# One bank and half the queries for the levels, value products by turns, context tables made earlier

## The chip, the cores and the metric

The kernel runs on one NeuronCore of a Trainium2 chip. The metric is the device time in microseconds, as a median of several executions. The engines named are PE (TensorE, matrix products; PEld is its load of the stationary operand), DVE (VectorE), ACT (ScalarE), POOL (GpSimd) and SP (SyncE, which here only issues transfers). PSUM has eight banks of 128 partitions x 512 fp32 values; the code calls them `ps[:, bank, :]`.

## The reference

What is computed is two blocks on 512 tokens of width 1024. Cut to what matters here:

```python
def first_block(x, c, ctx, ...):
    px = split(modulate(rms_norm(x, norm1), sh1, sc1) @ w_in)       # q, k, v; q, f_fwd, f_bwd, i, g
    pc = split(modulate(rms_norm(ctx, norm1), csh1, csc1) @ w_in)   # the same of 256 context tokens
    na_x = neighbourhood_attention(...)   # 8 heads of 64; window of 8 rows x 16 columns, bias by
                                          # relative offset, one softmax with all context keys
    hg_x = hgrn2_mixer(...)               # 4 heads of 128, forward and backward in time
    x = x + gt1 * (concat(na_x, hg_x) @ w_out)
    return rms_norm(x + gt2 * peer_ffn(modulate(rms_norm(x, norm2), sh2, sc2), ...), norm_f)

def second_block(x, ...):                 # stick-breaking and latent attention, 8 heads each
    proj = (rmsnorm(x, norm_gain) * (1.0 + scale) + shift) @ w_in
    ...

# hgrn2_mixer, per head and direction: decayed linear attention, from a state that the context left
A = einsum('btd,bsd,btsd->bts', q, k, exp(b_t - b_s))   # for s <= t (or >=, backward)
o = A @ v + (q * exp(b)) @ S0                           # S0 = sum over context of k_dec^T v
```

## The kernel before

The program has four functions that run one after the other, each a block of queues for the five engines: `phase_project` (modulation, norm, all projections; 0 to 285 us), `phase_mix` (window attention and the recurrent mixer; 285 to 496), `phase_peer` (output projection, norm, the feed-forward with product keys, the final norm; 496 to 1834), and `second_block` (to the end at 2325). Activations are kept transposed, features on partitions and tokens along the row. Large products are made as three products in fp32r: `split3` (lines 1115 to 1117) multiplies high by high, low by high, high by low part; ScalarE makes the high part, VectorE or POOL the low part. Small ones are plain fp32.

**`phase_project`** streams 32 pieces of the weights; a piece is 8 k-steps of `split3`. The last pieces are those of the gates `g`, whose products ScalarE's sigmoid and VectorE's product (line 413) finish.

**`phase_mix`** has two strands. The attention has 32 items (a head, a block of 16 columns x 8 rows; two heads of a pair follow each other). An item is `scores` (lines 729, 730: 256 window keys, 256 context keys), DVE's bias and maxima (`item`, lines 941, 945), ACT's exponential (894) and scaling (898), `turn` (738: four transposes into bank 2), ACT's copy to `pT` (922), `values` (750: four 64-column products into one half of bank 3). The recurrent strand has four units, `unit` = head pair and direction `d`; a unit has ten levels 0 to 9 and a `read_out`. Level 0 is the diagonal. At level s from 1 to 7 (`LEV`) the tokens of each tile of 128 are cut in runs of 2^(s-1); a query in a later run of a pair meets the keys of the earlier one, through `qd` (made by DVE, line 997), `kd` (POOL, 716) and the running factors `suf` and `fx` (DVE, 1003, 1007). TensorE makes the whole 128x128 matrix for each of 4 tiles and 2 heads (`level`, line 791, one bank a head, 4 and 5), and DVE copies the valid part of it into `A_diag` under a mask (`copied`, 966). Levels 8 and 9 mix whole tiles (808 and below). TensorE's product of level s waits for the copy of level s-1 (`level_cp`), head by head.

Ahead of unit 0 stands, for each direction, `context(d)`: eight transposes of the context's decayed keys `k.fc[d]` (759), ACT's copy to `kcT` (905), eight products with the context's values (765) to the state, ACT's copy of it (908). Three bias tables of 128x2048 (one for the left edge, the inner blocks, the right edge) are made from `k.toep` and `k.mask`: DVE makes the first (1037) and POOL the other two (699).

The order of the mix is set by slots: slot n holds `scores(n)`, then a share of the recurrent steps, spread evenly by `fill` over 36 slots, then `turn(n-2)` and `values(n-3)`. Every engine has the same slots in its queue.

**`phase_peer`** first makes the output projection (`out_part`, banks 0 to 7), adds squares for the norm, and spreads the reciprocal root (`spread_quarters`, line 1131) over the partitions; then groups of two tiles follow, `OUT_G` = 4 the first after the norm. DVE makes h of the norm (1626, 1622) k-step by k-step, which the first tile of group `OUT_G` waits for (`h_split`). After that group TensorE turns h (1412, 1413) and waits for the weights' low part of POOL (1331). At its end DVE adds residuals and squares for the next norm (1800).

**`second_block`** begins with the same kind of norm (`n_inverse`, `n_spread`; h by lines 2416 and 2422), then projects tile by tile from weight pieces (ACT line 2180 high, DVE 2311 low). The rotary angles (`rope_angles`, line 2365) lie in DVE's queue ahead of a low part.

## Time and profile before

| | us |
|---|---|
| median of 3 runs | 2329.17 (2326.9 to 2331.43) |
| the profiled execution | 2327.29 |
| its span on the core | 2325.5, mean clock granted to TensorE 0.977 |
| TensorE busy | 2196.0 (94%) |
| VectorE busy | 1664.4 (72%) |
| ScalarE busy | 908.7 (39%) |
| POOL busy | 624.9 (27%) |

A row of a timeline is: start in us, duration in us, engine, line, operation, out<-in, shapes, xcount (consecutive ones joined), and in brackets the idle time of the engine before it and what ended that. A row by lines is: line, engine, operation, names, shapes, xcount | busy us, mean ns of one | idle us before them and who ended it. A row of a table by stretches is: the stretch in us, its length, busy us of PE, PEld, DVE, ACT and POOL with the number of instructions in brackets, the granted clock of TensorE as a share of full, the share of the DMA engines, GB/s. A product of plain fp32 is two records.

### The profile page before, as it was taken

To read this page: it belongs to the slowest core of one execution; us is meant where nothing else is said; L and a number is where in the kernel's file an instruction comes from. 1 tells how busy PE (TensorE), PEld (TensorE's weight loads), DVE (VectorE), ACT (ScalarE), POOL (GpSimd) and SP (SyncE) were. 2 spreads that over 40 slices of the span, in tenths; PEclk is the share of its full clock that TensorE was granted. 3 is DMA by queue.
4 is the path that set the end of the run, shared out by engine and by line. 5 is a ranking of instruction groups with operands and counts; after the bars stand their busy time and mean duration, and the time that the engine had idled before them with its cause. 6 is when DMAs were issued, how large, how long until landed. Compare 5 with 4: busy or idle time off the path is not lost. (4 is left out here: it accounts for less than half of the span.)

```text
span 2325.5 us, 31686 instructions
## 1 busy us (share of the span) xinstructions
PE 2196.0 (94%) x12605; PEld 1961.9 (84%) x12605; DVE 1664.4 (72%) x2779; ACT 908.7 (39%) x1191; POOL 624.9 (27%) x355
## 2 busy tenths in 40 slices
PE   5999889988999998999999899999999899889997
PEld 3888777866799998999999899999999777667775
DVE  6645677873479999889886788888887645656543
ACT  3322234343233333566663333333333434556432
POOL 0000042322347776333325333333332000000000
PEclk8999999999999999999999999999999999999999
DMA  7677400012237777899999999999998122111222
GB/s 263 216 235 240 163 33 1 1 73 73 91 115 244 248 241 235 314 357 339 353 356 385 356 359 352 358 355 352 359 353 308 68 82 90 55 42 55 78 90 73
DMA packets 177443, 486.13 MB, mean 209 GB/s; under 512 B 13648, under 2 KB 80336, under 8 KB 165776
## 3 DMA queue, kind: packets, MB, share of 16 engines
q1 hardware_dynamic: 140432, 349.87, 43.6%
q0 software_dynamic: 36864, 134.23, 15.5%
q8 instruction: 100, 1.64, 0.3%
q14 instruction: 47, 0.39, 0.0%
HBM read 429.52 MB, written 52.43 MB: 207 GB/s over the span
## 5 line engine op out<-in xcount | busy, mean ns | idle before, releaser
L1115 PE MATMUL ps<-h_high,u_high 128*128 128x384 f32 (+1 forms) x1216 | 427.7, 352 | 19.9 <-POOL u_low L1331 12.4
L1117 PE MATMUL ps<-h_high,u_low 128*128 128x384 f32 (+1 forms) x1216 | 419.7, 345 | 0.0
L1116 PE MATMUL ps<-h_low,u_high 128*128 128x384 f32 (+1 forms) x1216 | 419.6, 345 | 0.0
L1115 PE MATMUL ps<-w_high,v_high 128*128 128x384 f32 x1024 | 344.5, 336 | 7.5 <-DVE w_low L1750 7.5
L1117 PE MATMUL ps<-w_high,v_low 128*128 128x384 f32 x1024 | 343.8, 336 | 0.0
L1116 PE MATMUL ps<-w_low,v_high 128*128 128x384 f32 x1024 | 343.6, 336 | 0.0
L1115 PEld LDWEIGHTS ps<-h_high,u_high 128*128 128x128 f32 x1216 | 230.3, 189 | 33.9 <-POOL u_low L1331 14.6
L1481 ACT ACTIVATE v_high<-v_raw 128x2048 fp32r<-128x2048 f32 x64 | 122.6, 1916 | 347.9 <-PE ps L1117 341.2
L1115 PE MATMUL ps<-h_high,w_high 128*128 128x512 f32 x560 | 226.4, 404 | 17.1 <-DVE h_low L2422 5.1
L1117 PEld LDWEIGHTS ps<-h_high,u_low 128*128 128x128 f32 x1216 | 229.9, 189 | 8.0
L1116 PEld LDWEIGHTS ps<-h_low,u_high 128*128 128x128 f32 x1216 | 230.5, 190 | 7.1
L1116 PE MATMUL ps<-h_low,w_high 128*128 128x512 f32 x560 | 221.2, 395 | 0.0
L1117 PE MATMUL ps<-h_high,w_low 128*128 128x512 f32 x560 | 220.8, 394 | 0.0
L1738 DVE TENSOR_TENSOR v_low<-v_raw,v_high 128x2048 fp32r<-128x2048 f32 x64 | 146.7, 2292 | 98.6 <-ACT v_high L1481 98.6
L1319 POOL DMA_INDIRECT mixT<-in_peer_v,row_index x102 | 146.9, 1440 | 241.2 <-DVE row_sum L1783 224.4
L1319 POOL DMA_INDIRECT mixT<-in_peer_u,row_index x103 | 145.7, 1414 | 233.7 <-DVE row_dot L1708 212.7
L1115 PEld LDWEIGHTS ps<-w_high,v_high 128*128 128x128 f32 x1024 | 193.7, 189 | 8.1 <-DVE v_low L1738 5.5
L1116 PEld LDWEIGHTS ps<-w_low,v_high 128*128 128x128 f32 x1024 | 193.5, 189 | 0.0
L1117 PEld LDWEIGHTS ps<-w_high,v_low 128*128 128x128 f32 x1024 | 193.4, 189 | 0.0
L1557 ACT ACTIVATE gelu<-ps 128x384 f32<-128x384 f32 x128 | 62.9, 492 | 314.4 <-PE ps L1117 312.6
L2311 DVE TENSOR_TENSOR w_low<-w_raw,w_high 128x1024 fp32r<-128x1024 f32 x64 | 78.3, 1223 | 98.8 <-ACT w_high L2180 98.7
L1115 PEld LDWEIGHTS ps<-h_high,w_high 128*128 128x128 f32 x560 | 107.0, 191 | 48.4 <-issue 8.0
(437 smaller groups left out, 4153.7 us busy)
## 6 DMA issues: line engine op xcount, KB each, us to landing
v_raw<-in_peer_v SPq DMA_DIRECT2D x64, 1024.0 KB, 6.4
w_raw<-in_w SPq DMA_DIRECT2D x94, 512.0 KB, 3.6
u_first<-in_uT SPq DMA_DIRECT2D x32, 1024.0 KB, 5.9
u_second<-in_uT SPq DMA_DIRECT2D x32, 1024.0 KB, 5.9
xT<-in_late_w SPq DMA_DIRECT2D x56, 512.0 KB, 4.4
gelu_up<-gelu SPq DMA_DIRECT2D x128, 192.0 KB, 6.3
gates<-gates_sb SPq DMA_DIRECT2D x12, 2048.0 KB, 9.9
weighted<-gelu_up SPq DMA_DIRECT2D x64, 384.0 KB, 6.7
```

The costliest lines, as they stand in the source:

```text
L1115: pe.matmul(out, wh, mh, start=start, stop=False)
L1116: pe.matmul(out, wh, ml, start=False, stop=False)
L1117: return pe.matmul(out, wl, mh, start=False, stop=stop)
L1319: pool.indirect_dma_start(out=row_of(total), out_offset=None, in_=table, in_offset=bass.IndirectOffsetOnAxis(ap=row_no[:, n:n + 1], axis=0))\
L1481: act.activation(v_high[:, g % 2], v_raw[:, g % 2], ACT.Copy).then_inc(v_hi, 1)
L1557: act.activation(gel[:, x % 4, :], ps[:, x % 4, 0:DENSE], ACT.Gelu).then_inc(u_ev, 1)
L1738: dve.tensor_tensor(v_low[:, g % 2], v_raw[:, g % 2], v_high[:, g % 2].bitcast(F32), ALU.subtract)\
L2311: dve.tensor_tensor(wlo[:, i % SPLITS, :], raw[:, i % RAWS, :], whi[:, i % SPLITS, :].bitcast(F32), ALU.subtract).then_inc(w_low, 1)
```

## The change

It has seven parts.

1. The context's turning and states leave the mix. `turn_context(d)` and `states(d)` stand in project's queue of TensorE: the first turning after the third piece from the end, the first states and the second turning after the last but one, the second states after the last. The steps `ctx` leave the mix's slots (45 steps in place of 47).
2. The bias tables are made in project: the inner and the right one by POOL, the left one by DVE as its last instruction. The first table, `kcT` and the states lie in `k.xT`, which is free then. So SP loads `xT` again only at the end of the mix, behind the weights `u_first`.
3. Levels 1 to 7: TensorE streams only the 64 later queries of each tile, both heads into one bank (4 or 5 by turns), waits for the copy of level s-2, and DVE makes one masked copy of 512 elements.
4. The value products of two items are made together, their halves of the array by turns, and `pT` has three buffers.
5. `idle_products` (fp32 products of ones and zeros into a bank that is not in use) stand ahead of the first out part of `phase_peer`, around its norm's spread, and around the one of the second block.
6. Group `OUT_G` of `phase_peer` makes both of its tiles k-step by k-step; two of the final squares are added after the last residual.
7. In the second block the rotary inputs are loaded after three weight pieces, POOL makes the low part of the second piece, and the first two tiles are interleaved by `FIRST_STEPS` (two k-steps of each, then one of each at a time, then the last three of each).

```diff
@@ phase_project
+            pool.wait_ge(proj, ctx_done)
+            pool.wait_ge(k.table_in, 32)
+            for v in (1, 2):
+                pool.tensor_tensor(k.bias[v]..., k.toep..., k.mask[:, v, :]..., ALU.add)
...
+            dve.wait_ge(k.table_in, 32)
+            dve.tensor_tensor(k.bias[0]..., k.toep..., k.mask[:, 0, :]..., ALU.add)
...
+            def turn_context(d):
+                pe.wait_ge(ctx_keys, 2)
+                ...
+                        last = pe.transpose(ps[:, bank, ...], k.fc[d][:, h, j * P:(j + 1) * P], k.ident[:])
+            def states(d):
+                bank_free(J + 3 * d + 2)
+                pe.wait_ge(turned_c_sb, d + 1)
+                ...
+                if p > turn_at[0]:
+                    states(p - turn_at[1])
+                if p in turn_at:
+                    turn_context(p - turn_at[0])
@@ phase_mix
+            sp.dma_start(k.u_first[:], k.dram["w_out_g"][0]).then_inc(k.u_in[0], 16)
             xv = k.dram["xT"].rearrange("(k p) t -> p k t", p=P)
+            sp.wait_ge(maxed, 2 * N)
+            sp.wait_ge(av, HP * HG)
             for h in range(2):
                 sp.dma_start(k.xT[:, 4 * h:4 * h + 4, :], xv[:, 4 * h:4 * h + 4, :]).then_inc(k.load_x[h], 16)
...
+            def values(pair):
+                pe.wait_ge(turned_sb, 2 * pair + 2)
+                ...
                 for j in range(4):
+                    for i in (2 * pair, 2 * pair + 1):
+                        ...
+                        last = pe.matmul(ps[a:a + DH, 3, 0:P], v, pT[:, i % WEIGHTS_T, j * P:(j + 1) * P],
+                                         start=j == 0, stop=j == 3)
...
+                elif s <= LEV:
+                    pe.wait_ge(level_cp, n_cp(unit, max(s - 2, 0)))
+                    for h in range(HP):
+                        for i in range(TILES):
+                            asked = half_of(q[:, h, i * P:(i + 1) * P], s, 1 - d)
+                            at = (TILES * h + i) * LATER
+                            last = pe.matmul(ps[:, 4 + s % 2, at:at + LATER], key[:, h, i * P:(i + 1) * P], asked,
+                                             start=True, stop=True)
...
+                src = ps[:, 4 + s % 2, :].rearrange("p (i n m) -> p i n m", i=HP * TILES, m=m)
+                into = A[:].rearrange("p i (n two m) -> p i n two m", two=2, m=m)[:, :, :, 1 - d, :]
+                dve.copy_predicated(into, own, src).then_inc(level_cp, 1)
@@ phase_peer
+            idle_products(pe, k, ps[:, 3, :], 4)
             for x in range(3):
                 pe.wait_ge(u_split, PIECES_BEFORE + x // GE + 1)
...
+            idle_products(pe, k, ps[:, 4, :], 2)
             pe.wait_ge(e_inverse, 1)
             spread_quarters(pe, k, ps[:, 6, :], rt[:]).then_inc(e_spread, 1)
+            idle_products(pe, k, ps[:, 4, :], 2)
...
+                if g == OUT_G:
+                    ...
+                    for t in range(KT):
+                        pe.wait_ge(h_split, OUT_TILES + t + 1)
+                        for j in range(GE):
+                            last = up_part(j, t)
...
-                if n >= 2:
+                if 2 <= n < KT - 2:
                     link(add_squares(n - 1))
+            for n in (KT - 3, KT - 2):
+                link(add_squares(n))
@@ second_block
+                if i == RAWS:
+                    sp.dma_start(pos_i[RS], k.dram["positions"]...)
...
+            pool.wait_ge(w_high, 2)
+            pool.wait_ge(w_low, 1)
+            pool.tensor_tensor(wlo[:, 1, :], raw[:, 1, :], whi[:, 1, :].bitcast(F32), ALU.subtract).then_inc(w_low, 1)
...
+            idle_products(pe, k, ps[:, 3, :], 3)
             pe.wait_ge(n_inverse, 1)
             spread_quarters(pe, k, ps[:, 2, :], rt_q).then_inc(n_spread, 1)
+            idle_products(pe, k, ps[:, 3, :], 3)
+            for j, steps in FIRST_STEPS:
+                ...
```

TensorE's queue at the border of project and mix. Before (line 759 turns the context's keys, 765 makes the states, 791 is a level, 729 and 730 are an item's scores):

```order
L118 UNCONDITIONAL_BRANCH
L719 UNCONDITIONAL_BRANCH
L729 MATMUL ps<-kT,qT 128x256
L730 MATMUL ps<-kT,qT 128x256
L759 MATMUL ps<-ident,u_first 128x128 x8
L765 MATMUL ps<-ic,qd 128x128 x8
L759 MATMUL ps<-ident,u_first 128x128 x8
L765 MATMUL ps<-ic,qd 128x128 x8
L729 MATMUL ps<-kT,qT 128x256
L730 MATMUL ps<-kT,qT 128x256
L791 MATMUL ps<-hq,kk 128x128 x8
```

The same place after (line 591 makes the states, 777 and 778 the scores, 821 is level 0 and 830 level 1):

```order
L591 MATMUL ps<-ic,xT 128x128 x8
L118 UNCONDITIONAL_BRANCH
L767 UNCONDITIONAL_BRANCH
L777 MATMUL ps<-kT,qT 128x256
L778 MATMUL ps<-kT,qT 128x256
L821 MATMUL ps<-hq,kk 128x128 x8
L830 MATMUL ps<-qd,kd 128x64 x8
```

Turning and states stand ahead of the border now, and level 0 follows the first score pair.

TensorE's queue in the second unit, two slots. Before (738 turns an item's weights, 750 are its value products):

```order
L791 MATMUL ps<-qd,kd 128x128 x8
L738 MATMUL ps<-ident,s_sb 128x128 x4
L750 MATMUL ps<-w_raw,vw 64x128 x2
L750 MATMUL ps<-w_raw,vc 64x128 x2
L729 MATMUL ps<-kT,qT 128x256
L730 MATMUL ps<-kT,qT 128x256
L791 MATMUL ps<-qd,kd 128x128 x16
L738 MATMUL ps<-ident,s_sb 128x128 x4
L750 MATMUL ps<-w_raw,vw 64x128 x2
L750 MATMUL ps<-w_raw,vc 64x128 x2
```

After:

```order
L830 MATMUL ps<-qd,kd 128x64 x8
L786 MATMUL ps<-ident,s_sb 128x128 x4
L777 MATMUL ps<-kT,qT 128x256
L778 MATMUL ps<-kT,qT 128x256
L830 MATMUL ps<-qd,kd 128x64 x16
L786 MATMUL ps<-ident,s_sb 128x128 x4
L798 MATMUL ps<-w_raw,vw 64x128 x4
L798 MATMUL ps<-w_raw,vc 64x128 x4
```

The level products have 64 columns, and value products stand in every other slot, eight in a row for two items.

DVE's queue in the same unit, one slot with a level of runs of 8, ahead of it the copies of the level before. Before:

```order
L966 COPY_PREDICATED A_diag<-pred,ps 128x512 x2
L941 ISA s_sb,na_max<-ps,bias 128x256
L941 ISA na_max 128x1
L945 ISA s_sb,na_max<-ps,zeros 128x256
L945 ISA na_max 128x1
L948 TENSOR_REDUCE na_max<-na_max 128x1
L952 RECIPROCAL na_sums<-na_sums 128x1
L997 TENSOR_TENSOR qd<-hq,fx 128x64x8
L1003 TENSOR_TENSOR suf<-suf,fx 128x64x8
L1007 TENSOR_TENSOR fx<-fx 128x64x8
L966 COPY_PREDICATED A_diag<-pred,ps 128x512 x2
```

After:

```order
L991 COPY_PREDICATED A_diag<-pred,ps 128x256x2
L962 ISA s_sb,na_max<-ps,bias 128x256
L962 ISA na_max 128x1
L966 ISA s_sb,na_max<-ps,zeros 128x256
L966 ISA na_max 128x1
L969 TENSOR_REDUCE na_max<-na_max 128x1
L973 RECIPROCAL na_sums<-na_sums 128x1
L1018 TENSOR_TENSOR qd<-hq,fx 128x64x8
L1024 TENSOR_TENSOR suf<-suf,fx 128x64x8
L1028 TENSOR_TENSOR fx<-fx 128x64x8
L991 COPY_PREDICATED A_diag<-pred,ps 128x128x4
```

Two copies have become one; the order around them is the same.

## Rows read from the trace of the kernel before

**Rows 1.** A table by stretches, middle of the mix.

```profile
340.00:396.00 56.00, 53.71 (x359) 44.28 (x360) 36.91 (x97) 21.20 (x45) 14.89 (x10) 1.00 0.00 1
```

**Rows 2.** The timeline of TensorE in the mix, one slot with one level.

```profile
352.93 0.70 PE L729 MATMUL ps<-kT,qT 64*128 64x256 f32 x2
...
356.40 0.65 PE L750 MATMUL ps<-w_raw,vw 128*64 128x128 f32 x4
...
357.42 0.70 PE L729 MATMUL ps<-kT,qT 64*128 64x256 f32 x2
```

**Rows 3.** Groups by line in the mix, 300 to 500 us.

```profile
L791 PE MATMUL ps<-qd,kd 128*128 128x128 f32 x448 | 58.7, 286 | 8.8 <-DVE A_diag L966 7.1 <-DVE A_diag L963 1.7
...
L966 DVE COPY_PREDICATED A_diag<-pred,ps 128x512 f32<-128x512 uint8 x56 | 37.5, 721 | 1.0
...
L997 DVE TENSOR_TENSOR qd<-hq,fx 128x512 f32<-128x512 f32 x34 | 22.9, 673 | 0.0
```

**Rows 4.** The timeline at the start of the mix.

```profile
285.38 2.29 DVE L1037 TENSOR_TENSOR bias<-w_raw,win_mask 128x2048 f32<-128x2048 f32 x1 [0.32 <-PEq L118]
...
287.75 9.48 POOL L699 TENSOR_TENSOR bias<-w_raw,win_mask 128x2048 f32<-128x2048 f32 x2 [1.46 <-DVE bias L1037]
...
288.59 4.24 DVE L988 TENSOR_SCALAR kk<-fx 128x1024 f32<-128x1024 f32 x1
...
298.99 2.05 PE L791 MATMUL ps<-hq,kk 128*128 128x128 f32 x16
```

**Rows 5.** The same timeline, context turning and states of the second direction.

```profile
293.80 1.04 PE L759 MATMUL ps<-ident,u_first 128*128 128x128 f32 x8
...
295.95 2.05 PE L765 MATMUL ps<-ic,qd 128*128 128x128 f32 x16 [1.11 <-ACT qd L905]
```

**Rows 6.** In project: a timeline row of the loads, and the stretch around them.

```profile
32.78 0.97 PEld L516 LDWEIGHTS ps<-group_sum,hgate 128*128 128x128 f32 x8 [1.62 <-ACT hgate L438]
...
32.70:33.90 1.20, 1.05 (x8) 0.97 (x8) 1.20 (x4) 0.03 (x1) 0.00 (x0) 1.00 1.08 413
```

**Rows 7.** The timeline of TensorE in the second block, value products.

```profile
1991.93 1.09 PE L2132 MATMUL ps<-at_wT,sqkv 128*64 128x128 f32 x16
```

**Rows 8.** The timeline at the start of `phase_peer`.

```profile
516.81 1.47 DVE L1587 TENSOR_TENSOR h_low<-mixT,h_high 128x512 fp32r<-128x512 f32 x2
...
517.25 0.39 PE L1115 MATMUL ps<-h_high,u_high 128*128 128x512 f32 x1
...
517.93 0.39 PE L1115 MATMUL ps<-h_high,u_high 128*128 128x512 f32 x1
```

**Rows 9.** The timeline around the feed-forward's norm and group OUT_G.

```profile
555.98 1.78 PE L1131 MATMUL ps<-c_root,ident 128*128 128x128 f32 x8 [1.74 <-DVE c_root L1617]
...
560.23 0.77 PE L1115 MATMUL ps<-h_high,u_high 128*128 128x512 f32 x1 [2.47 <-DVE h_low L1622]
...
569.99 4.61 POOL L1331 TENSOR_TENSOR u_low<-u_second,u_high 128x2048 fp32r<-128x2048 f32 x1 [21.78 <-ACT u_high L1475]
...
575.20 0.38 PE L1412 MATMUL ps<-ident,h_high 128*128 128x128 f32 x2
...
578.69 0.48 PE L1115 MATMUL ps<-h_high,u_high 128*128 128x512 f32 x1
```

**Rows 10.** The timeline at the end of `phase_peer`.

```profile
1832.21 0.69 DVE L1800 TENSOR_TENSOR v_raw<-v_raw 128x512 f32<-128x512 f32 x1 [0.78 <-ACT v_raw L1573]
```

**Rows 11.** The timeline at the start of the second block.

```profile
1842.52 0.76 PE L1115 MATMUL ps<-h_high,w_high 128*128 128x512 f32 x1 [4.13 <-DVE h_low L2422]
...
1861.29 1.23 DVE L2311 TENSOR_TENSOR w_low<-w_raw,w_high 128x1024 fp32r<-128x1024 f32 x1
```

**Rows 12.** The timeline in project, a low part on POOL.

```profile
40.53 2.51 POOL L295 TENSOR_TENSOR w_low<-w_raw,w_high 128x1024 fp32r<-128x1024 f32 x1 [38.59 <-DVE w_low L351]
...
40.87 2.72 DVE L343 TENSOR_TENSOR h_low<-xT,h_high 128x512 fp32r<-128x512 f32 x1
```

**Rows 13.** The table by stretches, around level 1 of the first unit.

```profile
303.00:306.00 3.00, 2.18 (x10) 2.21 (x11) 3.00 (x3) 0.00 (x0) 2.16 (x1) 0.62 0.00 0
```

More of the change, by code:

```diff
@@ L861, in _ @@
                     turn(n - 2)
-                if 0 <= n - 3 < N:
-                    values(n - 3)
+                if 0 <= n - 3 < N and (n - 3) % 2:
+                    values((n - 3) // 2)
         @block.scalar
@@ L868, in copies @@
                 act.wait_ge(level_mm, n_mm(unit, s))
-                if unit == 0:
-                    act.wait_ge(table, 3)
                 if s == 8:
@@ L1117, in split3, with idle_products @@
     return pe.matmul(out, wl, mh, start=False, stop=stop)
+def idle_products(pe, k, out, count):
+    for _ in range(count):
+        pe.matmul(out, k.ones[:], k.zeros[:], start=True, stop=True)
 def quarter_sums(pe, k, out, squares, start, stop):
@@ L2536, in build @@
                 k.hgate = sb("hgate", [P, HG, T], where=na)
+                with ExitStack() as parts:
+                    k.hc = [sb(name, [P, KT, C], F32R, where=parts) for name in ("hc_high", "hc_low")]
+                tables = sb("bias", [P, 2, ROWS, NH, KB], where=na)
+                spare = k.xT[:].rearrange("p a t -> p (a t)")
+                k.bias = [spare[:, 0:2048].rearrange("p (a h m) -> p a h m", a=ROWS, h=NH), tables[:, 0], tables[:, 1]]
+                k.kcT = spare[:, 2048:3072].rearrange("p (n d) -> p n d", d=P)
+                k.state = spare[:, 3072:4096].rearrange("p (e h t) -> p e h t", e=2, h=HG)
                 phase_project(k)
```

224 lines of the change are left out of this document (110 added, 114 removed).

## The prediction

> **What bounds the kernel now.** I read the page first: TensorE is busy 94% of the span, so what counts is its gaps and its stages of small matrices. The stages come next, in a table of busy time by stretches. In the middle of `phase_mix` TensorE works 53.71 of 56 us at full clock, VectorE only 36.91 [rows 1]: this stage is bound by TensorE, and a step taken from VectorE or ScalarE gives time there only where TensorE waits for it. A slot with one level runs from one pair of score products to the next, 352.93 to 357.42, 4.49 us [rows 2]: scores 1.05, level 1.78 (16 records of 0.111: each fp32 product is two records), turning the weights 0.64, value products 1.02 (356.40 to 357.42). The groups by line tell what TensorE waits for in this phase: 8.8 us ahead of the level products, 7.1 of it for VectorE's masked copy [rows 3]. Last I went through the borders of the phases in the timeline, where TensorE idles and then runs at half clock.
>
> **Part 1: start of the mix.** Before, VectorE's last gate of `phase_project` ends at 285.06 (0.32 ahead of its first instruction of the mix at 285.38) and level 0 of the first unit at 298.99 [rows 4]. Between stand two score pairs and both directions of context turning, which wait for ScalarE copies and these for ScalarE's queue. The change puts 8 transposes and 8 state products for each direction into TensorE's queue around the last two pieces. What of this lies ahead of the last projection's gate: turning 0.95 (8 records in 1.04, the last of which overlaps what follows), the first states 1.85 (16 records in 2.05, likewise), turning 0.95 [rows 5], 3.8 us; the second states run beside the gate. So the gate ends at 288.9. VectorE then makes table 0, 2.29 us [rows 4], now ahead of the block's end: 291.2; block change 0.3; one score pair 1.05: level 0 at 292.6, 6.4 earlier. One score pair of that is only moved behind it, so 5.3. Against it stand the first levels, which now come before their operands: `kk` (1.3 us if POOL is quiet, as twice a half-width product's 0.67 [rows 3]; 4.24 beside POOL's table, [rows 4]) and two full-width `kd` on POOL lie ahead of level 1 and 2, and TensorE has only a score pair between them. I take 1.2 off: **4.1**. POOL's two tables, 9.48 us, run in project beside VectorE's work there; what they delay is VectorE's low parts of the next pieces, made two pieces ahead, and the 24 products of a piece, 5.4 us at 0.227, hide that; if that cover is gone they cost up to 5. SyncE's x load, moved to the end of the mix, stands there behind the last maxima and read-outs and nothing of the mix waits for it; it now comes ahead of weight pieces of `phase_peer`, whose first ones were loaded long before.
>
> **Part 2: levels with half the columns.** TensorE: 448 of its records now stream 64 columns instead of 128. This sounds like the main part of the change, and I put it at **zero**. Products of the same stationary size, with only 2 moving columns, stand in the trace: 8 records of line 516 take 0.97 from the first start to the last end, (0.97 - 0.19)/7 = 0.112 each, at clock 1.00 [rows 6]. That is the level's 0.111. The load of a 128x128 fp32 matrix sets this pace, not the columns. By the Trainium skill, "TensorE: Matmul & The Clock Gate", section "LDWEIGHTS (loading the stationary operand)", a load takes its columns/1.2 ns, 107 for 128, and the row agrees. The same page's section "Back-to-back issue gap" gives, for a sustained stream, a smaller spacing at 128 columns than at 512, by which fewer columns would shorten records; that is a rival below.
> VectorE: one copy of 512 elements instead of two (1.34 a level, 37.5 us for 56) saves 0.67 in each of 28 levels, off the path. What is on the path is the wait: now the product of level s needs only the copy of level s-2, since banks 4 and 5 alternate, and of TensorE's 8.8 us of waits [rows 3] I keep those at the units' starts and take **5** as gained. Runs of 1 and 2 elements as the moving operand have no row; VectorE's half-width products at all strides (line 997, mean 673) show no price of strides [rows 3]; I take zero and bound it by a doubled record in the first two levels of four units, 8 x 16 x 0.11 = 14.
>
> **Part 3: value products by turns.** Line 750's records are loads of 64 columns, but each takes 0.11 to 0.13, 8 of them 1.02 [rows 2]. In the second block the same shape already goes by turns between two halves of the array, 16 records in 1.09, 0.055 to 0.068 each [rows 7]. A pair of items so takes 16 x 0.066 = 1.06 instead of 2.04: 0.98 saved, 16 pairs, **15.7**. It is on the path wherever TensorE is the bound: a slot of one level then needs 4.0 on the mean, VectorE 3.7 (three half-width products for queries, suffix and factors at 0.67 to 0.69, a copy at 0.67 to 0.72 [rows 3], and 1.02 for an item's maxima and reciprocal). The bound holds, with little to spare. Mix: 4.1 + 5 + 15.7 = **24.8**.
>
> **Part 4: start and out-projection of `phase_peer`.** Idle products stand ahead of the first out part, which TensorE begins after a wait; first products after a wait take 0.77 instead of 0.39 (half clock, as at 560.23 [rows 9]), and some such products would be quicker. But TensorE is caught there by VectorE, whose low parts of x=0, t=6 and 7 end at 517.54 and 518.28, about when TensorE comes to them (517.25 and 517.93) [rows 8]: **0** (-1 to +1.3). At the feed-forward's norm the spread takes 1.78 for 8 records, half clock; after two idle products some 0.9. First product at 559.4 instead of 560.23. From there the first group makes both its tiles k-step by k-step: 16 x 0.68 [rows 8] = 10.9 us of TensorE work, which covers VectorE's making of h; before, tile one paced by VectorE and then tile two end at 575.20, then h is turned, 3.5, and the next group starts at 578.69. POOL's low part is there at 574.58 at the latest [rows 9]. Now: 559.4 + 10.9 + 3.5 = 573.8, near POOL's end: gain **4.9** (3 to 5.2).
>
> **Part 5: end of `phase_peer`.** Two squares are put behind the last residual; the last ones wait 0.78 for ScalarE and take 0.69 [rows 10]. Behind the last residual there is one more short step and not this idle: **0.7**.
>
> **Part 6: second block.** Raw pieces are asked for ahead of the rope rows (1.2 earlier), idle products take off the half clock of the first products (0.76, after 4.13 idle [rows 11]), and tiles 0 and 1 are interleaved: TensorE would be 1 to 2 us earlier. Against it: POOL now makes the second low part beside VectorE. Where this happens in project, POOL's takes 2.51 and VectorE's low part, that starts 0.34 later, takes 2.72 and not 0.7 [rows 12]. The Trainium skill, "SBUF — State Buffer", section "Who interferes with whom", has a lock on a port pair that both share; these two rows agree with it. VectorE's first low part of h so comes some 2 us late, and it is what TensorE waits for. And all of it meets tile 3, whose low part of the weights is made behind the rope angles (starts at 1861.29, [rows 11]): about 1863.8 in either case. **-0.3** (-2 to +2).
>
> **Sum.** 24.8 + 0 + 4.9 + 0.7 - 0.3 = 30.1. The profiled execution took 2327.3 (span 2325.5 and 1.8 around it), 1.9 under the median: 2297.2, so about **2299** as a median.
>
> **The rivals.**
> *Columns count (0.08).* In the stream of `phase_peer` three records of 512 columns take 0.68 (517.25 to 517.93, [rows 8]), 0.227 each; 64 columns would be an eighth of that, 0.028, and 448 of them 12.5 us less on TensorE. VectorE's 3.7 a slot then binds, so only some 6 come: 2293. Against it speaks [rows 6]. The section "Back-to-back issue gap" of the Trainium skill, "TensorE: Matmul & The Clock Gate", speaks for it.
> *The turns don't overlap here (0.07).* In the mix both heads' results go to one bank, and the operands come by scores and turns between them: 15.7 is lost: 2315.
> *TensorE is granted less clock in the level stages (0.13).* Products with half the columns may not hold the upper level of the clock, 2.4 GHz, as the whole ones do [rows 1]. After a wait the clock in the mix was 0.62 over 303 to 306 [rows 13], so this stage can lose it; against it, [rows 6] held 1.00 with 2 columns. At half clock a record costs about 0.2 instead of 0.11 (spread's 1.78 for 8, [rows 9]). If a tenth of the mix's 170 us of TensorE work (0.96 of the time from 299 to 496, less the values' gain) is at half clock, 2315 (0.07); the change turns to a loss when it is over a sixth, 30 us; at a quarter, 2340. This is the case on the other side, 0.06.
> *Given back in waits (0.10).* TensorE, 20 us quicker in the mix, meets VectorE and POOL in slots of two levels: VectorE 6.5 against TensorE's 6.8, and POOL's `kd` is chained to VectorE's suffix in each level. A third of the gain goes: 2308.
> *Forecast as it stands (0.62)*: own range 2290 to 2306, from the bounds: start 0 to 5, copies 3 to 7, values 13 to 16, out group 3 to 5, second block -2 to +2. That a part does not do what it says (idle products that don't raise the clock) is inside it: 1.5.
>
> **Numbers.** A measurement of this kernel tells about 0.2% (4.7 us) from no change. Faster by more: 0.62 + 0.08 + 0.07 + 0.07 + 0.10 = 0.94, less 0.02 for a mishap that none of these names; within: 0.02; slower: 0.06. The range, 2289 to 2313, holds the forecast, the first and the last rival and half of what lies at 2315.
>
> **What would show it.** Right: level records at 0.11 with 64 columns; 16 value records in about 1.06; waits ahead of level products under 3 us; level 0 near 292.6; mix shorter by about 25; the group after the first of the feed-forward near its POOL part; second block unchanged to 1 us. Wrong: records of levels at 0.09 or 0.19, a granted clock under 0.9 in the middle of the mix, value records still at 0.11, or VectorE or POOL named ahead of level products by tens of us.

## The result, and the profile after

The changed kernel is slower: 2337.74 us (median of 15, 2333.39 to 2340.13) against 2331.0 (median of 15) for the kernel before, ratio 1.0029 with a 95% interval of 1.0022 to 1.0035. The forecast was 2299, the range 2289 to 2313. Its profiled execution took 2333.95 us, span 2332.1, TensorE's mean clock 0.970 (0.977 before), TensorE busy 2203.4 us (2196.0 before). Among the experiments below two single executions lie far off the rest (2475.45 us with the old levels, 8196.5 with the idle products alone); the medians of ten given there contain them and would be 2332.3 and 2324.4 without.

First the borders of the phases, since the sum was made phase by phase. VectorE's first instruction of `phase_peer` stands in the timeline of the kernel before, and then of after:

```profile
496.66 0.17 DVE L1579 SCALAR_TENSOR_TENSOR c_gain<-mod,cols 128x8 f32<-128x8 f32 x1 [10.86 <-PEq L615]
```

```profile
506.99 0.17 DVE L1616 SCALAR_TENSOR_TENSOR c_gain<-mod,cols 128x8 f32<-128x8 f32 x1 [9.76 <-PEq L674]
```

| | before | after | difference |
|---|---|---|---|
| first score product of the mix | 285.38 | 292.31 | +6.9 |
| length of the mix | 211.3 | 214.7 | +3.4 |
| length of `phase_peer` | 1337.1 | 1332.6 | -4.5 |
| second block | 491.8 | 492.5 | +0.7 |

The later border of project was forecast (291.5), and the last two lines nearly so (-5.6 and +0.3). By the forecast the mix should end 24.8 us earlier than before; it ends 10.3 later. Of the 36.8 us between the profiled execution and its forecast of 2297.2, 35.1 lie there.

The timeline of after around the start of the mix (answers to [rows 4, 5]):

```profile
288.28 1.95 PE L591 MATMUL ps<-ic,xT 128*128 128x128 f32 x16
289.72 2.28 DVE L452 TENSOR_TENSOR xT<-w_raw,win_mask 128x2048 f32<-128x2048 f32 x1
292.31 0.67 PE L777 MATMUL ps<-kT,qT 64*128 64x256 f32 x2 [2.08 <-PEq L118]
293.82 2.05 PE L821 MATMUL ps<-hq,kk 128*128 128x128 f32 x16 [0.41 <-DVE kk L1011]
...
297.13 0.69 DVE L1024 TENSOR_TENSOR suf<-suf,fx 128x512 f32<-128x512 f32 x1 [2.23 <-POOL kd L760]
298.58 1.29 DVE L982 TENSOR_TENSOR A_diag<-ps,ident 128x512 f32<-128x512 f32 x2
...
300.02 3.64 PE L830 MATMUL ps<-qd,kd 128*128 128x64 f32 x16 [4.15 <-DVE A_diag L982]
```

States, table and level 0 are where they were put (level 0 at 293.82, forecast 292.6). But level 1 starts only at 300.02. It waits for VectorE's copy of level 0 (line 982), which in VectorE's queue stands behind the suffix, and this waits for POOL's first full-width `kd`. And the 16 records of level 1 take 3.64 us, half clock. In the kernel before, level 1 started at 303.82, behind a wait too:

```profile
303.82 3.61 PE L791 MATMUL ps<-qd,kd 128*128 128x128 f32 x16 [1.72 <-DVE A_diag L963]
```

So level 1 comes 3.8 us earlier, but two pairs of scores (2.1 us) that stood ahead of it stand behind it now: 1.7 us gained where 4.1 were forecast. The wait grew from 1.72 to 4.15.

What follows is in the table by stretches of after (us, length, busy PE, PEld, DVE, ACT, POOL with counts, granted clock, DMA share, GB/s; answers to [rows 1, 13]):

```profile
300.00:345.00 45.00, 44.98 (x180) 37.98 (x180) 28.56 (x72) 12.15 (x26) 10.57 (x9) 0.50 0.00 1
345.00:404.00 59.00, 56.07 (x406) 45.51 (x404) 36.32 (x98) 24.08 (x51) 16.90 (x10) 0.99 0.00 1
404.00:416.00 12.00, 5.30 (x38) 4.50 (x39) 7.45 (x17) 4.18 (x8) 1.51 (x1) 0.72 0.00 0
416.00:445.00 29.00, 29.00 (x236) 24.59 (x235) 27.70 (x69) 14.07 (x29) 13.62 (x8) 1.00 0.01 2
449.00:455.00 6.00, 5.27 (x20) 4.12 (x22) 0.00 (x0) 2.07 (x4) 0.00 (x0) 0.50 0.00 0
```

For 45 us, nearly all of the first unit, TensorE is busy without a pause (44.98) and is granted 0.50, 1.2 GHz. The half clock ends at 346.6; behind it TensorE has 2.4 GHz with the same kind of products. Work of about 23 us was done in 46. In the profiled execution of before the clock had been back at 1.00 by 309, after two dips. Further on there are two more places, in the timeline of TensorE:

```profile
406.97 0.91 PE L1145 MATMUL ps<-mixT,ones 128*32 128x128 f32 x16 [3.00 <-ACT mixT L916]
410.73 3.78 PE L1153 MATMUL ps<-hq,ident 128*128 128x128 f32 x16 [2.85 <-DVE hq L1049]
...
449.73 3.75 PE L847 MATMUL ps<-qd,kd 128*128 128x256 f32 x8 [4.36 <-ACT w_raw L907]
```

Here the norm of the first head pair and a level 9 wait 3.00, 2.85 and 4.36 us. In the kernel before the same three wait 0.3, 0.2 and nothing.

The products themselves did what was forecast. TensorE's timeline of after in the third unit, at full clock (answers to [rows 2, 7]), and the groups by line of the mix (answer to [rows 3]):

```profile
421.15 0.66 PE L798 MATMUL ps<-w_raw,vw 128*64 128x128 f32 x8
421.64 0.61 PE L798 MATMUL ps<-w_raw,vc 128*64 128x128 f32 x8
422.18 0.70 PE L777 MATMUL ps<-kT,qT 64*128 64x256 f32 x2
...
423.23 2.00 PE L830 MATMUL ps<-qd,kd 128*128 128x64 f32 x16
```

```profile
L830 PE MATMUL ps<-qd,kd 128*128 128x64 f32 x448 | 66.5, 313 | 4.1 <-DVE A_diag L982 4.1
L991 DVE COPY_PREDICATED A_diag<-pred,ps 128x512 f32<-128x512 uint8 x28 | 24.9, 890 | 7.4 <-PE ps L830 6.6
```

Sixteen value records take 1.03 us by turns. A level of 64 columns takes 2.00 where one of 128 took 2.05 [rows 4]: the columns save nothing, at full clock. The waits ahead of level products went from 8.8 to 4.1, all of it at level 1.

### The profile page after: what moved, and what is told of

The parts are those of the page before. It is cut to its first block and busy times, and to the rows that moved or that the text cites. A ratio compares the mean times of both kernels' runs of the same rounds, so it can differ in the third digit from the quotient of the medians.

```text
span 2332.1 us, 31686 instructions
## 1 busy us (share of the span) xinstructions
PE 2203.4 (94%) x12633; PEld 1966.8 (84%) x12633; DVE 1661.7 (71%) x2750; ACT 909.2 (39%) x1193; POOL 625.0 (27%) x356
## 5 line engine op out<-in xcount | busy, mean ns | idle before, releaser
L1131 PEld LDWEIGHTS ps<-h_high,u_high 128*128 128x128 f32 x1216 | 230.1, 189 | 28.1 <-POOL u_low L1353 13.9
```

What stands on the lines that cost most here:

```text
L1131: pe.matmul(out, wh, mh, start=start, stop=False)
```

## The experiments

The kernels fall into three sets: parts of the change undone in after, parts done alone in before, and a measurement of the clock by itself. Ratios are to the kernel before, run on the same chip at the same time (its median was 2329.4 to 2330.7 there). "Mix" is the length of the mix in the profiled execution, "PE idle" the sum of TensorE's idle times by lines in it, the one ahead of its first product taken in. The medians are of ten executions, but of fifteen in the first two rows, of four in the kernels with former slots and idle products, of five in the last row.

| kernel | median us | ratio to before (95%) | mix | PE idle |
|---|---|---|---|---|
| before | 2331.0 | | 211.3 | 18.1 |
| after | 2337.7 | 1.0029 (1.0022 to 1.0035) | 214.7 | 23.1 |
| after, old levels | 2332.6 | 1.0005 (0.9993 to 1.0016) | 208.4 | 32.0 |
| after, former slots | 2321.3 | 0.9956 (0.9930 to 0.9981) | 202.5 | 16.8 |
| after, idle products | 2326.2 | 0.9985 (0.9966 to 1.0004) | 200.7 | 21.5 |
| after, former slots and idle products | 2310.7 | 0.9912 (0.9896 to 0.9929) | 187.2 | 16.4 |
| the same without turns | 2312.6 | 0.9923 (0.9904 to 0.9941) | 191.4 | 7.1 |
| the same, more idle products | 2307.6 | 0.9908 (0.9891 to 0.9924) | 186.5 | 13.4 |
| before, new levels | 2327.0 | 0.9989 (0.9978 to 1.0000) | 207.4 | 10.9 |
| before, turns | 2328.3 | 0.9992 (0.9982 to 1.0002) | 208.6 | 32.0 |
| before, both | 2326.6 | 0.9982 (0.9966 to 0.9998) | 220.7 | 19.0 |
| before, peer and second block | 2325.0 | 0.9983 (0.9973 to 0.9992) | 215.4 | 18.6 |
| all but parts 1 and 2, idle products | 2312.1 | 0.9917 (0.9900 to 0.9933) | 214.8 | 17.7 |

Some kernels scatter more than others from execution to execution (former slots alone: 2309.83 to 2332.75; before with both: 2316.92 to 2339.41), and there the mean granted clock falls as the time grows (0.979 at 2309.83, 0.968 at 2332.75). The three with former slots and idle products stay within 7 us each, and so does after (2333.39 to 2340.13), whose profiled execution lost the clock in its first unit.

The column "mix" is weaker evidence than the medians. The profiled execution was the slowest of its kernel in five of these rows: "before, both" (2339.41), "all but parts 1 and 2" (2329.36), "before, peer and second block" (2332.35), "the same without turns" (2316.16), and the row above that (2311.45); it was the fastest or second fastest in "before, new levels" (2321.61), "after, idle products" (2318.52) and after (2333.95). How much this matters shows in "before, peer and second block": its mix has the code of the kernel before and is 4.1 us longer. Differences of mix under about 4 us therefore show nothing by themselves.

### The old levels back in the changed kernel

```diff
-                elif s <= LEV:
-                    pe.wait_ge(level_cp, n_cp(unit, max(s - 2, 0)))
-                    ...      # 64 columns, both heads into bank 4 + s % 2
+                if s <= LEV:
+                    for h in range(HP):
+                        if s:
+                            pe.wait_ge(level_cp, n_cp(unit, s - 1, h))
+                        ...  # 128 columns, head h into bank 4 + h; two copies
```

> The changed kernel with levels 1 to 7 as before: 128 columns a product, one bank a head, two masked copies, the wait for the copy of the level before. Theory C (products with 64 columns do not bring the clock back once it is lost; the profile of after has 0.50 from 300 to 345 us with TensorE busy all the time): the clock is back at 1.00 by about 312 us, some 20 us of slow products go, some 5 of waits for copies return: 2322. Rival W (the clock stays low there for another reason, as the longer wait for level 1 or the value products by turns): the clock stays at 0.50 to about 345 and the waits come on top: 2342.

Measured: 2332.6. The clock was at half here too, from 292 on, and is back at 1.00 by 305, as theory C has it, though TensorE waits more here (38.94 busy of 45):

```profile
300.00:345.00 45.00, 38.94 (x266) 32.14 (x265) 34.43 (x90) 16.63 (x36) 14.06 (x10) 0.98 0.00 1
```

TensorE did 266 records in the time in which it did 180 in after. But the gain is 5 us and not 15: the waits for VectorE's copies ahead of level products come to 13.0 us in this kernel (8.8 before), and level 8 waits another 3.9.

### The former slots

```diff
-    steps = []
+    steps = [("ctx", d, 0) for d in range(2)]
...
     for x, step in enumerate(steps):
+        if step[0] == "ctx":
+            continue
         fill[min(x * (SLOTS_N - 1) // len(steps), SLOTS_N - 1)].append(step)
```

> The changed kernel with the recurrent steps in the slots that they had before the change (two empty steps ahead, so that each step counts as one of 47). Theory S (without the two context steps the norm of the first head pair and level 9 of units fell into other slots than the work that they wait for; TensorE idles 3.00 + 2.85 at 407 to 411, 4.36 at 450, 1.31 at 392, and runs 408 to 415 and 449 to 455 at half clock): these waits shrink to those of before (under 1 us each), 12 us gained: 2326. Rival (these waits come from TensorE being ahead of ScalarE and VectorE, whatever the slots): within 3 us of the changed kernel.

Measured: 2321.3, 16 us less than after (12 were expected). The norm now waits 1.5 in all (5.9 in after), the level 9 of the four units together 3.8 (6.1), and the half clock at 450 is gone. The first unit still goes at 0.50 from 300 to 340. So taking two steps out of a list of 47 that is spread evenly over 36 slots moved the others against the items, and this alone costs more than the 6.7 us that the whole change lost.

### Idle products ahead of level 1

```diff
                 else:
+                    if unit == 0 and s == 1:
+                        idle_products(pe, k, ps[:, 6, :], 4)
                     pe.wait_ge(q_ready, n_q(unit, s))
```

> The changed kernel with four idle products (fp32, 512 columns, into a free bank) ahead of level 1 of the first unit, where TensorE waits 4.15 us. Theory C: the clock is held through the wait, and the levels with 64 columns keep it, as they do in units 1 to 3: 1.00 from 300 to 345 us, some 20 us gained: 2317. Rival W' (64 columns in this unit lose the clock by themselves): it is at half again before 320, under 5 us gained.

Measured: 2326.2, 11.6 less than after. Neither theory had it right: the clock is held through the wait, level 1 takes 1.97 us, but at 311.17, after two gaps of 0.63 and 1.00 us ahead of the queries (`qd`), it falls, and is back at about 324. Half clock lasts some 13 us in place of 46.

```profile
308.16 2.01 PE L832 MATMUL ps<-qd,kd 128*128 128x64 f32 x16 [0.63 <-DVE qd L1020]
311.17 3.68 PE L832 MATMUL ps<-qd,kd 128*128 128x64 f32 x16 [1.00 <-DVE qd L1020]
```

### New levels alone in the kernel before

The edit is the reverse of the first one, in the kernel before.

> The kernel before with only levels 1 to 7 changed (64 columns, one bank, one copy, the wait for level s-2). Theory C: the dips of the clock that the kernel before has at 303 to 308 us (0.62 to 0.84) are not made good within the first unit, which then runs at half clock to its read-out: 15 to 20 us lost, 5 won from the waits: 2344. If 64 columns regain the clock as 128 do: 2326. If they shorten the records: 2320 or less.

Measured: 2327.0, 3.7 us less than before, where theory C expected 13 more. The dip came (7.06 us for the 32 records at 303.95), and the half clock lasted to 320 and not to the unit's end: shorter than after's. It is longer than in before's own profile, but not than in the profile of "before, peer and second block", whose mix is that of before, with 128 columns. There the second and third level of the first unit run at half clock, to 318.9:

```profile
309.44 3.75 PE L791 MATMUL ps<-qd,kd 128*128 128x128 f32 x16 [1.45 <-DVE A_diag L966]
...
315.98 3.50 PE L791 MATMUL ps<-qd,kd 128*128 128x128 f32 x16
```

So in the kernel before, old and new levels don't clearly differ in how long the clock stays low: 12.9 us with 128 columns, 15 with 64, one profile each. Products of 64 columns thus can stand in a stretch in which the clock rises. "They never bring it back" was too strong; what was still open was whether the columns had a part in it at all. The waits ahead of levels fell from 8.8 to 2.4 us, the 5 us of the prediction and more; in time 3.7 came of it, with an interval that reaches to no gain.

### The columns by themselves

To have little differ but the columns, the products of level 1 of the first unit are made twelve times more, right behind their long wait: 96 products, 192 records. Nothing reads them. The first kernel has 64 columns (every second one, as level 1 has), the second 128, the third 64 that are neighbours. The edits differ in one thing more: with 64 columns all results go to one bank, with 128 to two.

```diff
                     pe.wait_ge(level_cp, n_cp(unit, max(s - 2, 0)))
+                    for r in range(12 if (unit, s) == (0, 1) else 0):
+                        for h in range(HP):
+                            for i in range(TILES):
+                                at = (TILES * h + i) * LATER
+                                pe.matmul(ps[:, 6, at:at + LATER], key[:, h, i * P:(i + 1) * P],
+                                          half_of(q[:, h, i * P:(i + 1) * P], s, 1 - d), start=True, stop=True)
+                                # second: ps[:, 6 + h, i * P:(i + 1) * P], ..., q[:, h, i * P:(i + 1) * P]
+                                # third: the first, with q[:, h, i * P:i * P + LATER]
```

> The changed kernel, and right ahead of level 1 of the first unit, behind its long wait, the products of that level twelve times more with 64 columns each (96 products, 192 records, into a free bank; nothing reads them). Theory C (64 columns don't bring the clock back): all 192 records run at half clock, 0.23 us each, some 43 us, granted clock 0.50 to their end. If they do bring it back: 0.23 for the first few, then 0.111, some 22 us in all. The time as a whole is that of after plus this.

> The same with 128 columns in each of the 96 added products (into two free banks), behind the same wait. Theory C: the clock is back at 1.00 within some 8 us, as in the run with the old levels, and the 192 records take 0.111 from there, some 25 us in all; and if the clock then holds, unit 0 of this kernel is 20 us shorter than that of after. If the columns don't matter for the clock: the same picture as with 64 columns.

> As the run with the level's products twelve times more at 64 columns, but the 64 columns are neighbours, not every second one (level 1 has runs of one element). If it is the number of columns that keeps the clock down: half clock to the end of the 192 added records, 41 us, as with every second one. If it is the reading in steps of two elements: the clock is back within some 4 us, as with 128 columns, and they take 23 us.

Measured 2376.9, 2340.5 and 2377.9 (one execution each). The added records in TensorE's timeline, in the order of the three kernels:

```profile
299.44 41.19 PE L830 MATMUL ps<-qd,kd 128*128 128x64 f32 x192 [3.23 <-DVE A_diag L988]
```

```profile
299.25 23.02 PE L829 MATMUL ps<-qd,kd 128*128 128x128 f32 x192 [2.25 <-DVE A_diag L987]
```

```profile
300.09 41.19 PE L830 MATMUL ps<-qd,kd 128*128 128x64 f32 x192 [4.15 <-DVE A_diag L988]
```

and the stretch from 300 to 310 of the first and the second:

```profile
300.00:310.00 10.00, 10.00 (x49) 10.00 (x48) 2.58 (x4) 0.82 (x2) 0.18 (x1) 0.50 0.01 2
```

```profile
300.00:310.00 10.00, 10.00 (x83) 10.00 (x82) 2.40 (x3) 0.81 (x2) 0.00 (x1) 0.90 0.01 2
```

With 128 columns the clock, at half from the start of the mix on in this execution, is back within some 2 us of 300 and stays to 390; the 192 records take 23.02 us. With 64 they take 41.19, all at half clock, and the half clock goes on to 386 or 387 through the unit behind them. The kernel with 23 us of more work of twice the columns ends 2.8 us behind the median of after, so the rest of it is some 20 us shorter. The stride has no part: neighbours give the same 41.19.

This is theory C at this place, as far as one execution of each kernel goes. Two things besides the columns differ. The wait ahead was 2.25 us with 128 columns, 3.23 and 4.15 with 64; against the wait as the reason speaks the kernel with former slots, which waited 1.87 us ahead of its 64-column levels and stayed at half clock to 340. The other is the bank: 64 columns into two banks, or 128 into one, was not run, and it differs in the same way between after and after with the old levels. So either the columns or the single bank keeps the clock down; that it is the columns is not shown.

How it fits the run before, where 64-column levels didn't hold the clock down to the unit's end, isn't shown either. The traces have a hint. In every profile in which a unit of 64-column levels ran at half clock, the clock came back beside value products: in after at 346.6, and likewise in the kernels with former slots (340.4), with idle products (323.7) and with the new levels alone (320), never within a stretch of level records alone. Not every set of value products brought it back: in after one at 332 did not. From the timeline of after:

```profile
331.99 1.12 PE L798 MATMUL ps<-w_raw,vw 128*64 128x128 f32 x8
...
345.22 1.12 PE L798 MATMUL ps<-w_raw,vw 128*64 128x128 f32 x8
346.13 0.84 PE L798 MATMUL ps<-w_raw,vc 128*64 128x128 f32 x8
346.89 0.70 PE L777 MATMUL ps<-kT,qT 64*128 64x256 f32 x2
```

### Both losses mended

The two edits of "former slots" and "idle products" together.

> The changed kernel with both: recurrent steps in their former slots, and four idle products ahead of level 1 of the first unit. If the two losses stand side by side, the mix (202.5 us with the slots alone, 200.7 with the idle products alone, 214.7 in after) comes to about 189, the whole to 2303. If the clock of the first unit decides and falls in the small gaps of its levels whatever is ahead of them, the mix stays at 200 and the whole at 2318.

Measured: 2310.7, 27 us under after and 0.88% (0.71 to 1.04) under the kernel before. The two losses stand side by side: the former slots gain 16.4 without the idle products and 15.5 with them, the idle products 11.6 and 10.6; the mix is 187.2 (189 expected). The clock is at 1.00 from 300 to 335:

```profile
300.00:335.00 35.00, 30.96 (x217) 24.56 (x216) 31.24 (x76) 14.59 (x31) 16.17 (x10) 1.00 0.00 1
```

The whole was placed 8 us too low, 5 of them because `phase_peer` and the second block came out that much longer in this profile than in after's.

Then further idle products in the same unit: one ahead of level 0, one ahead of level 9, two ahead of the read-out, each within the wait that stands there.

> The changed kernel with former slots, four idle products ahead of level 1, and further ones in the other waits of the first unit: one ahead of level 0 (waits 1.62 there), one ahead of level 9 (1.48), two ahead of the read-out (1.98). If the clock is then held through the first unit, the 4 us of slow products that are left there (293 to 300 and 335 to 338) go by half: 2308. If more products only lengthen TensorE's queue: 2311.

Measured: 2307.6, as expected by the first of the two; its four executions (2306.19 to 2309.69) overlap those of the kernel above, so that the gain of this step is not shown. It has the lowest median of the study.

### The turns

Value products by turns in the kernel before; then after with former slots and idle products, and the value products item by item again.

```diff
-            def values(i):
-                ...
-                for j in range(4):
-                    last = pe.matmul(ps[a:a + DH, 3, 0:P], v, pT[:, i % 2, j * P:(j + 1) * P], ...)
+            def values(pair):
+                ...
+                for j in range(4):
+                    for i in (2 * pair, 2 * pair + 1):
+                        last = pe.matmul(ps[a:a + DH, 3, 0:P], v, pT[:, i % WEIGHTS_T, j * P:(j + 1) * P], ...)
```

> The kernel before with the value products of a pair by turns, and nothing else. Theory (TensorE bounds the mix; records go from 0.11 to 0.066): 15.7 us less: 2315. Rival (the chain of VectorE's copies, s-1 ahead of s, takes over: idle time ahead of the level products grows from 8.8 us to the 13 of the run with old levels and more): 2321.

> The changed kernel with former slots and four idle products (2310.7), but the value products item by item again. It tells what the turns are worth beside the new levels: with TensorE the bound of the mix, 15.7 less 1 to 2: 2325. If VectorE's steps of each slot bind as they do with the old levels (where the turns alone gave 1.8): 2313.

Measured: 2328.3 for the turns alone, 1.8 less than its 2330.1 of before and not to be told from it; 2312.6 without them against 2310.7 with them, four executions each that overlap. The forecast was 15.7. Groups by line of the mix, the level products in the kernel with the turns alone (8.8 in [rows 3]), then in the one with former slots and idle products without turns, and in the one with them:

```profile
L793 PE MATMUL ps<-qd,kd 128*128 128x128 f32 x448 | 58.1, 284 | 17.7 <-DVE A_diag L968 15.5 <-DVE A_diag L965 2.2
```

```profile
L833 PE MATMUL ps<-qd,kd 128*128 128x64 f32 x448 | 54.3, 276 | 0.0
...
L865 PE MATMUL ps<-qd,xT 128*128 128x512 f32 x15 | 8.1, 618 | 1.6 <-ACT w_raw L913 1.6
```

```profile
L834 PE MATMUL ps<-qd,kd 128*128 128x64 f32 x448 | 54.8, 277 | 1.6 <-POOL kd L766 1.0 <-DVE qd L1022 0.5
...
L866 PE MATMUL ps<-qd,xT 128*128 128x512 f32 x16 | 8.5, 614 | 2.8 <-ACT w_raw L914 2.8
L851 PE MATMUL ps<-qd,kd 128*128 128x256 f32 x32 | 7.9, 388 | 4.7 <-ACT w_raw L911 4.7
```

With the old levels the copies of VectorE take the place of the products: idle time in the mix goes from 18.1 to 32.0 us, 13.9 of 15.7. With the new levels it is ScalarE's copies of levels 8 and 9 that now end the waits: idle time 16.4 against 7.1, and the mix is 4.2 us shorter and not 15.7. In the kernel without turns no level from 1 to 7 waits and level 9 waits 0.5 us in all: there TensorE bounds the mix.

### Levels and turns in the kernel before

> The kernel before with levels of 64 columns and value products by turns, the context's turning still in the mix. If the two add up (3.9 us of mix of the one, 15.7 of the other): 2311. If a slot that is shorter on TensorE leaves gaps in which the clock falls again and 64 columns are slow to bring it back, as in after: the half-clock stretch of the first unit is longer than the 17 us of the run with the levels alone, and the whole comes to 2322.

Measured: 2326.6, with one of the two widest scatters, 2316.92 to 2339.41. Its profile is of the slowest execution: half clock from 305 to 345, and again from 370 to 390. That the two add up to 2311 is refuted; the other case named what this profile shows, and 5 us too little of it. What an execution of the median does isn't shown. The second stretch begins behind a wait of only 1.08 us, for POOL's `kd` ahead of a level of the second unit, so it isn't the first unit alone that can lose the clock. The profile also shows that the loss needs neither the moved context nor the moved slots.

### All but the moved context

Everything but parts 1 and 2, and two idle products ahead of level 1.

> Everything of the change but parts 1 and 2 (turning, states and tables stay in the mix, and with them the former slots), and two idle products ahead of level 1 of the first unit, where TensorE waits some 2 us. Beside the run with former slots and idle products (2310.7) it tells what parts 1 and 2 are worth: by the prediction's 4.1, 2315. If the clock falls here in the gaps of the start (ScalarE copies between turning and states) and the first unit goes at half: 2325.

Measured: 2312.1 (four of five between 2308.68 and 2313.79; the fifth, 2329.36, is the profiled one, with half clock in two units, from 313 to 340 and from 364 to 384). Beside 2310.7 parts 1 and 2 are worth 1.4, within the scatter, where 4.1 were forecast; the idle products are two here and four there.

### Peer and second block alone

> The kernel before with only the edits of phase_peer and of the second block. By the prediction's sum 0 + 4.9 + 0.7 - 0.3 = 5.3 us less: 2325.5; the profile of after has 4.5 less in phase_peer and 0.7 more in the second block, which gives 2327.

Measured: 2325.0, ratio 0.9983 (0.9973 to 0.9992), 5.2 less than its 2330.1 of before, where the sum had 5.3. Its profiled execution is the slowest and can't tell how the 5.2 are shared.

## Why the prediction was wrong

**What decided was a rival.** "TensorE is granted less clock in the level stages" had 0.13, and 0.06 for a loss; its point of decision, a sixth of the mix's work at half clock, was reached: 23 us of work in the first unit and 5 behind the later waits, some 28 of 170. The sum had no term for the clock at all: part 2 priced the new levels at zero, by the duration of a record at full clock. That is the step that cost most, these 28 us beside a miss of 35 in the mix. Three more failed: the start, the slots and the value products.

**The row against the rival was read for too much.** I held that [rows 6] stayed at 1.00 with 2 columns, so that few columns do no harm. This row is 1.2 us long, behind a wait of 1.62. It shows the duration of a record at full clock, and for that it was right (2.00 us a level in after). It says nothing of 45 us of such records behind a wait. The dip to 0.62 of [rows 13] was the row to go by: it said that there is a wait at this very place, and how much slower a level is behind it. I took it as a sign that the stage can lose the clock, and never asked what brings it back. What the runs showed in its place: idle products ahead of level 1 gain 11.6 us without the former slots and 10.6 with them.

**The start.** 1.2 us were taken off for operands that come late; the wait ahead of level 1 was 4.15 (1.72 before), and 1.7 us were gained by level 1 in place of 4.1. The order of VectorE's queue (suffix before the copy of level 0) and POOL's `kd` would have given it: `kk` at 293.7, `kd` 2.36 us as in the trace of before, suffix and factors 1.4, copy 1.3, some 299; with the 3.18 that `kd` took in after, 299.8.

**The slots.** It was plain from the code that 47 steps became 45 and that `fill` spreads them evenly. I costed the two steps that left and not the moves of the others. The norm of the first pair and level 9 lost 10 us in waits and their half clock; the run with former slots measures this at 16.

**Value products by turns: the term was mis-sized.** The record price was right (1.03 for 16). "The bound holds, with little to spare" was not: it compared busy times per slot (4.0 against 3.7), while what releases TensorE is a chain, the product, the copy, the next product, and for levels 8 and 9 a copy of ScalarE. Measured worth: 1.8 and 1.9 us by the medians of the two pairs, 4.2 by the length of the mix in two profiles.

**Smaller slips in the working.** For "columns count", 0.028 times 448 is 12.5 us of duration; the saving against 0.111 would be 37, and the 6 us of that rival rest on VectorE alone. The bounds given for the range add up to a gain of 17 to 35 us, 2294 to 2312, not 2290 to 2306. In the out group, POOL's low part was put at 574.58 at the latest, 0.8 later than the 573.8 on which the gain of 4.9 rests.

**Right:** half the columns do not shorten a level's records by more than the 2.05 to 2.00 us seen; waits for copies, 5 forecast, 6.4 found with the new levels alone. In `phase_peer`, the group `OUT_G` (timeline of after, answers to [rows 9]):

```profile
570.54 0.47 PE L1131 MATMUL ps<-h_high,u_high 128*128 128x512 f32 x1 [0.75 <-DVE h_low L1659]
...
580.30 4.55 POOL L1353 TENSOR_TENSOR u_low<-u_second,u_high 128x2048 fp32r<-128x2048 f32 x1 [21.17 <-ACT u_high L1512]
...
581.54 0.38 PE L1437 MATMUL ps<-ident,h_high 128*128 128x128 f32 x2
...
585.03 0.48 PE L1131 MATMUL ps<-h_high,u_high 128*128 128x512 f32 x1
```

From its first product to the turning it takes 11.0 (10.9 forecast), and 14.5 to the next group in place of 18.5: 4.0 of the 4.9. The missing 0.9 lies ahead of it: the spread takes 1.15 in place of 1.78, but starts later, and the group's first product stands 63.6 us behind the start of the phase in both kernels. Of the end of `phase_peer` (0.7 forecast) some 0.5 is left of the 4.5 by which the phase is shorter. In the second block, POOL's low part beside VectorE's first one (answers to [rows 12]):

```profile
1846.04 2.34 POOL L2079 TENSOR_TENSOR w_low<-w_raw,w_high 128x1024 fp32r<-128x1024 f32 x1 [5.87 <-ACT w_high L2235]
1846.16 2.76 DVE L2481 SCALAR_TENSOR_TENSOR h_low<-mqkv,ada,h_high 128x512 fp32r<-128x512 f32 x1
1849.07 0.77 PE L1131 MATMUL ps<-h_high,w_high 128*128 128x512 f32 x1 [3.19 <-DVE h_low L2481]
```

VectorE's low part takes 2.76 in place of 0.74 for the ones behind it, TensorE waits 3.19 for it and starts at half clock (0.77 for its first product) in spite of the idle products, 9.5 us into the block in place of 8.8. This is what the Trainium skill, "SBUF — State Buffer", section "Who interferes with whom", has for an instruction of VectorE with two SBUF inputs beside a reading one of POOL; these rows agree. What the interleaved tiles gained by themselves no run tells.

## What to carry to other kernels

Ahead of a stage of small products, look in the profile for the granted clock behind each wait and for how long it stays low, not only for the waits: here the same kind of stage ran at half clock for 46 us or at full clock from 300 to 335, by what stood ahead of it, and idle products put into a wait were worth more (11.6 and 10.6 us) than any part or group of parts of the change that was measured by itself (5.2 at most). If a list of steps is spread evenly over a loop, taking out steps moves every other one; keep the places and see first what the rest does. And where two engines hand work to and fro, compare the chain from release to release, not busy times.

## What the runs showed of the hardware that was not expected

- At the same place, behind waits of 3.23 and 4.15 us, 192 records of 128x128 fp32 loads with 64 moving columns into one bank ran at a granted clock of 0.50 from first to last (41.19 us, twice); with 128 columns into two banks, behind 2.25 us, at 1.00 from about 302 us on (23.02 us). At full clock 16 such records took 2.00 us in after and 2.05 before.
- A stage can be busy for 45 us without a gap (44.98 us) and stay at 1.2 GHz all the time, and in later units hold 2.4 GHz with the same products (1.00 from 346.6 to 404). In two other profiles the second unit lost the clock too, behind waits of 1.08 and 1.09 us.
- Some kernels with such a stage scatter by 20 us between executions (2309.83 to 2332.75 with the former slots), while the kernel before stayed within 8 (2325.16 to 2333.12). After, with the stage at half clock in its profile, stayed within 7.
